# Selections of a layer's first token group moved between the first expert's gate/up products

## The reference, cut to what matters

```python
lg = (xt @ wg + bg)                      # 4 groups; each token takes the best one
le = (xt @ we + be)                      # 4 experts in each group; top 2 of the chosen group
gates = ...                              # one weight per token and chosen expert
hu = einsum('td,edf->tef', xt, w_gate_up)   # 16 experts, 2048 -> 2 x 512
hg, hv = split(hu, 2)
act = silu(hg) * hv * gates
out = einsum('tef,efd->td', act, w_down)    # 512 -> 2048
```

## Time and profile before

| | us |
|---|---|
| median of three runs | 1507.21 |
| the profiled execution's own time | 1508.7 |
| its span in the trace | 1506.9 |
| TensorE busy in the span | 1397.0 (93%) |
| DMA queue of the weights (q1), share of 16 engines | 77.1% |
| chain that ended last: TensorE / DMA | 70% / 20% |

### The profile page before, as it was taken

One profiled execution on the slowest core, in us unless ns is written; L12 is line 12 of the kernel. 1 busy time (PEld: TensorE's weight loads), 2 busy tenths in 40 slices (PEclk: granted clock), 3 DMA queues, 4 the chain that ended last, 5 costly groups with the idle time before them and its releaser, 6 DMA issues.

```text
span 1506.9 us, 20710 instructions
## 1 busy us (share of the span) xinstructions
PE 1397.0 (93%) x9050; PEld 775.1 (51%) x9050; DVE 509.8 (34%) x1075; ACT 355.9 (24%) x549; POOL 21.7 (1%) x33
## 2 busy tenths in 40 slices
PE   6999999899899999999898988889999899899894
PEld 6999998899653333343243337654343233224331
DVE  5776776543432021022003026633014003103202
ACT  4556556432310120020012011320012012002000
POOL 0000000000000000000000000000000000000000
PEclk8999999999899999999999999989999999999997
DMA  9856453744579999999999995559999999999992
GB/s 301 247 161 189 135 174 103 233 168 168 185 297 422 428 408 429 427 426 429 429 425 429 426 361 207 202 156 399 427 427 428 426 428 427 427 426 428 425 428 91
DMA packets 94183, 495.42 MB, mean 329 GB/s; under 512 B 7533, under 2 KB 63789, under 8 KB 65869
## 3 DMA queue, kind: packets, MB, share of 16 engines
q1 hardware_dynamic: 84320, 466.11, 77.1%
q10 hardware_dynamic: 7098, 12.77, 2.9%
q0 software_dynamic: 2672, 15.21, 2.5%
HBM read 481.95 MB, written 16.04 MB: 330 GB/s over the span
## 4 chain that ended last, share of the span: by engine, by line
PE 70%; DMA 20%; DVE 5%; ACT 2%; issue 2%; ACTq 0%; SPq 0%; DVEq 0%; POOL 0%; POOLq 0%
PE ps L1099 19%; PE ps L1116 18%; DMA ring<-in_moe_w_down 17%; PE ps L1028 5%; PE ps L895 4%; PE ps L896 4%; PE ps L897 4%; PE ps L979 2%; PE ps L980 2%; PE ps L981 2%; PE ps L1177 2%; PE ps L1053 2%; PE ps L909 2%; DMA ring<-in_lru_w_in 1%; DMA xtok<-x_rows,src_now 1%
## 5 line engine op out<-in xcount | busy, mean ns | idle before, releaser
L1099 PE MATMUL ps<-ring,xsel 128*64 128x512 f32 x2048 | 464.9, 605 | 20.6 <-DMA ring<-in_moe_w_gate_up 20.3
L1116 PE MATMUL ps<-ring,work 128*32 128x512 f32 x3072 | 346.2, 595 | 13.4 <-DMA ring<-in_moe_w_down 13.4
L1099 PEld LDWEIGHTS ps<-ring,xsel 128*64 128x64 f32 x2048 | 142.1, 139 | 315.0 <-issue 272.3
L1116 PEld LDWEIGHTS ps<-ring,work 128*32 128x32 f32 x3072 | 91.7, 109 | 225.0 <-issue 203.0
L1666 DVE SCALAR_TENSOR_TENSOR arena<-arena,ps 64x512 f32<-64x512 f32 x32 | 21.7, 679 | 510.1 <-ACT work L780 510.1
L895 PE MATMUL ps<-operands,whi 128*128 128x288 f32 x512 | 153.4, 300 | 3.3 <-DVE ring_lo L1262 3.3
L896 PE MATMUL ps<-ring_lo,whi 128*128 128x288 f32 x512 | 151.5, 296 | 0.0
L897 PE MATMUL ps<-operands,ring_lo 128*128 128x288 f32 x512 | 150.6, 294 | 0.0
L1262 DVE TENSOR_TENSOR ring_lo<-ring,whi 128x1024 fp32r<-128x1024 f32 x96 | 115.4, 1223 | 77.4 <-ACT whi L599 77.2
L599 ACT ACTIVATE whi<-ring 128x1024 fp32r<-128x1024 f32 x96 | 100.5, 1057 | 150.4 <-PE ps L897 84.6
L779 ACT ACTIVATE arena<-ps 64x512 f32<-64x512 f32 x32 | 18.9, 589 | 407.7 <-PE ps L1099 407.6
(11 more groups left out here) (323 smaller groups left out, 1132.4 us busy)
## 6 DMA issues: line engine op xcount, KB each, us to landing
ring<-in_moe_w_gate_up SPq DMA_DIRECT2D x128, 2048.0 KB, 19.6
ring<-in_moe_w_down SPq DMA_DIRECT2D x64, 2048.0 KB, 21.1
ring<-in_lru_w_in SPq DMA_DIRECT2D x16, 2048.0 KB, 10.2
ring<-in_lru_w_out SPq DMA_DIRECT2D x8, 2048.0 KB, 17.8
x_rows<-xtok ACTq DMA_DIRECT2D x4, 1024.0 KB, 3.9
ring<-in_pool_w SPq DMA_DIRECT2D x4, 1024.0 KB, 15.9
xtok<-in_x_prompt SPq DMA_DIRECT2D x2, 1024.0 KB, 9.0
ring<-in_lru_w_a SPq DMA_DIRECT2D x8, 256.0 KB, 5.7
```

What stands on the lines that cost most here:

```text
L1099: last = mm(ps[half * ES:(half + 1) * ES, e % 2, :], xsel[:, k, e * ES:(e + 1) * ES], wt[:, half * 512:(half + 1) * 512], start=(k == 0), ...
L1116: last = mm(ps[rows:rows + QB, 2 + r, :], act[:, e % 2, f * W + slots0:f * W + slots0 + QB], wt[:, d * 512:(d + 1) * 512], start=start, st ...
```

## The change

The eight selections of a layer's first window are no longer issued ahead of the window. They stand at the places of `OWN_AT`, as in the last window: pairs 0 and 1 before part 0, pair 2 before part 2, pair 3 before part 4, and so on to pair 7 before part 12. The wait on `act_ready` that pairs 0 and 1 have in the last window is left out in the first one. The table itself is unchanged. Nothing changes on the other engines.

```diff
@@ -1035,8 +1035,6 @@
                 if l == 0:
                     eng.wait_ge(cstT_ready, 1)
                 stay_awake(8)
-                for q in range(PAIRS):
-                    select_rows(0, q)
 
                 def window(w, first=False, own=False, ahead=False):
                     seq = w if l == 0 else w + pe_extra[0]
@@ -1076,9 +1074,9 @@
                             turn_spread()
                         if i in TURN_ACT_AT:
                             turn_act(TURN_ACT_AT[i])
-                        if own and i in OWN_AT:
+                        if (own or first) and i in OWN_AT:
                             for r in OWN_AT[i]:
-                                if r < 2:
+                                if r < 2 and not first:
                                     eng.wait_ge(act_ready[l], w * (NE + 1) + (r - 1))
                                 select_rows(w, r)
```

## The result

Twenty executions of the changed kernel have a median of 1515.4 us, twenty of the kernel before on the same chip 1511.35 us. The ratio is 1.0036 [1.0025, 1.0046], so the change costs some 5.4 us (the difference of the means; the two medians lie 4.1 us apart). The profiled execution's own time is 1512.22 us (span 1510.4), against 1508.7 (1506.9) before.

The account below looks back on a forecast made before the run. TensorE bounds layer 0 up to the issue at 542.26, then transfers; transfers bound layer 1 from its first free slot. Layer 0 +2.7 and layer 1 -3.0 sum to -0.3 us: 1506.9 us forecast, 8-in-10 range 1502.5 to 1511.5.

Parts of the forecast that it names:

- The interleaving costs 1.17 us: First window, layer 0: six selections among parts of another tile shape take 1.365 us each; 1.3 us taken for layer 1.
- 1.55 us of stall: Layer 0, at `turn_act(0)`: TensorE arrives at 441.7 and waits to 443.25 for expert 0's gating; 0.5 us in layer 1.
- The chain: VectorE's `overflow` and one-hots in layer 0, after pair 7's copy: start 434.2 instead of 423.57, 7.51 us long, end 441.7.
- Layer 0: +2.7 us: At 542.26 TensorE frees the slot 2.7 us later with the DMA queue dry, and all transfers behind move with it.
- drop at the places: Layer 0, 446 to 454 us: granted clock 0.57 while and after TensorE does the many small products of the places.
- tight issue: Weight chunk issue with least room: layer 0 at 542.26, queue dry, 2.7 us later; layer 1 at 1130 us, lead kept.
- Layer 1: -3.0 us: Layer 1's MoE gets shorter by 3.0 us, as transfers set its pace and keep the lead won at the start.
- lead of 3.0 us: Layer 1's first chunks: earlier issues land weights 5.5 us sooner, shrinking to 3.0 by the fourth, then kept in a full queue.
- the forecast's own rule: Landing of 2 MB weight chunks: 7.5 us after issue into an empty queue, 4.9 us per chunk in a full one.
- 3.2 us of slack: Layer 1's tightest chunk, issued at 1130 us: what it could spare against an empty queue, 3.4 us, taken as 3.2.
- The slower one: Rival: stall at `turn_act(0)` widens layer 0's clock drop by 3.3 us, layer 1 gets one; +5.2, 1512.4 us, chance 0.13.
- that layer's fall alone: Case of the slower rival with the clock falling in layer 1 only: sum +1.9, 1509.1 us, chance 0.10.

Follow-up runs that it names:

- e5: The change plus four large products of no use ahead of the overflow counts in each layer; 1.0032 against the kernel before.
- e1: The change in layer 0 only, layer 1 keeping the old order; 1.0020 against the kernel before, +3.0 us.
- e9: The change with gates, counts and VectorE's overflow chain ahead of the selections, and three filler products instead of eight in layer 0; 0.9945 against the kernel before.
- e11: The old order with selections in one block, gates, counts and VectorE's overflow chain ahead, and the short filler in layer 0; 0.9958 against the kernel before.
- e7: The change with gates and counts moved ahead of the first selections; 0.9972 against the kernel before, where the old order with the same move has 0.9979.
- e2: The change in layer 1 only, layer 0 keeping the old order; 1.0029 against the kernel before, +4.4 us.
- e3: The change with the gates before part 5 instead of 1 and the counts before part 9 instead of 3; 1.0007 against the kernel before.
- e4: The change with VectorE's one-hot tiles moved behind expert 0's gating; 1.0030 against the kernel before.

## Why the prediction was wrong

It said 1506.9 us, no measurable change; it is 1515.4. 4.1 us of the 8.5 is the kernel before, whose median was 1507.21 over three runs and is 1511.35 over twenty. The other 4.4 are the change itself: -0.3 forecast, +4.1 between the medians, +5.4 by the ratio.

- **"The interleaving costs 1.17 us": right.** 1.2 us in e5.
- **"1.55 us of stall" in layer 0, 0.5 in layer 1: right in place, too large.** 0.99 us and none. The chain started at 435.15, not 434.2, since TensorE was later, and for the same reason TensorE reached line 1051 only at 443.0.
- **"Layer 0: +2.7 us": right in size, not shown in mechanism.** e1 has +3.0 [1.4, 4.7], the trace +3.3. But in that trace the fall behind the counts (1.7 us) and the missing drop at the places (3.3 us) nearly cancel with the 2.2 us of interleaving and stall. The tight issue at 542.44 is 1.0 us late, and the other 2.3 us arise behind it.
- **"Layer 1: -3.0 us": this is the step that failed.** The forecast let TensorE keep its pace through expert 0's products, put a fall of the clock behind the counts at nothing, and so banked a lead of 3.0 us from the first issues. The issues were forecast at -5.5, -2.8, -0.1 and +1.3 us. Counted from the layer's start they came at 42.0, 50.7, 57.0 and 61.8 us, against 46.9, 50.3, 53.8 and 57.2 before: -4.9, +0.4, +3.2 and +4.6. The 3.5 us that the low clock takes between 1009 and 1016 us stand in the last three. By the forecast's own rule (7.5 us into an empty queue, 4.9 behind the one before in a full one) the third lands at 64.5 and the fourth at 69.4, where the old order, at 4.9 us from 54.4, has it at 69.1. The lead is gone by then. A second low stretch costs 1.7 us (8.78 against 7.09 at 1042.97), and the tight issue comes 167.6 us after the start instead of 164.5, TensorE having lost 5.8 us (those 3.1 and the 2.7 of waits saved) rather than the 1.8 of the forecast. The 3.2 us of slack are used up: +1.0 at the end. With the gates and counts ahead and the clock up, e9 against e11 has the forecast's issues within 0.1 us and -2.7 us in layer 1, so in that pair of traces the rule for the lead held, and what the forecast lacked was the clock term.
- **The rivals.** The slower one named the clock and a time of 1512.4 for both layers, but put the fall at the places, with the stall as its cause. In layer 0 the places got no worse (1.00 between 446 and 454 us); layer 1 did get a fall there, the 1.7 us named above. The larger fall is at the counts, with no idle time in the 3.5 us (layer 0) and 7 us (layer 1) ahead of it, and e7 keeps the stall without the loss. The chances given to a costlier clock, 0.23 together, were too low. For a fall in layer 1 it left a lead of 0.8 us, so a sum of +1.9 for that layer's fall alone; e2 is at +4.4 [1.8, 7.0] with the change in layer 1 only. It missed that the fall comes before the lead is banked.

The Trainium skill's page TensorE: Matmul & The Clock Gate, in HAM oscillation — how this bites in real kernels, ties the return to the lower clock to idle gaps of the engine. The 4.58 us wait ahead of 997.53 agrees: the first selections behind it take 3.80 us, not 2.25. Behind the counts this case's trace shows the fall with no gap at all, so the measurement goes beyond the page.

**What was shown and what was not.** Shown by times: the loss needs the gates and counts at parts 1 and 3 (e7 and e3 against the change), and the stall isn't its cause (e4, e7). Gates and counts were moved together each time, so which of the two it needs was not separated. Shown by the clocks of all executions: the granted clock is lower with the new order beside the counts, by about what the loss is worth, and the same in both orders with the counts ahead. Shown by traces: in layers with the new order and the counts before part 3, the clock fell behind them in four of six (change, e2, e4; e1 and e4 have one layer without); with the old order in one of four. Not shown: that the clock is all of the 6.5 us. The falls in the trace of the change make 5.2 us behind the counts, but each trace is one execution, and why the clock falls in one and not in the next stays open. That the place of the commoner falls is behind the counts rests on ten layers.

## What to carry to other kernels

Here a burst of very small products was where TensorE's clock fell. Before new work is put around such a burst, look at the granted clock behind it in the windows, and try it where the engine waits anyway, here ahead of the gather. One trace can mislead: compare the mean granted clock over many executions. A lead won in the DMA queue counts only once the next issues have kept it; add up several issues, not the first. And compare a rearrangement with and without its neighbour moved: the same interleaving cost 5.4 us beside the counts and nothing with them out of the way.

## What was not expected of the hardware

- The granted clock went to 0.51 (1.2 GHz) for 3.5 and 7 us while TensorE was shown 100% busy, right behind 18 records of products with four columns. In e5, with 2.05 us of large products ahead of them, it stayed at 1.00 in both layers of the one trace.
- In e9 the clock was already low when the selections began and stayed so: it was 0.50 for 8 us of dense selections and products, and the first eight records of selections took 3.76 us instead of 2.25.
- Executions of one kernel differ by 10 us (1512.22 to 1522.94 for the change), so three runs put the kernel before 4 us too low.
